# Gated mixer of a 13-stage block: the scores of two heads side by side over 64 rows each, in two banks of their own; squares moved to GpSimd

## The chip, the cores and the metric

One core of a Trainium2 chip runs the whole program. The metric is the device time of one execution in microseconds (us), a median over runs. One core has TensorE (PE: matmuls; PEld is its loading of weights), VectorE (DVE), ScalarE (ACT), GpSimd (POOL) and SyncE (SP, which only issues transfers here). Each engine works through its own list of instructions in order and waits on semaphores that others raise.

## The reference, cut to what matters

The model is two blocks of two layers on a stream of 256 tokens by 1024 features, all in float32: eight feed-forward stages, four mixers and one key/value stage. The change is in one mixer, the gated one (`mlstm`):

```
H, L = 8 heads, chunks of 64 tokens; q, k: 64 wide per head, v: 128 wide per head
q, k, v, ig, fg, og = split(h @ w_in);  q = q / 8
log_i = ig + b_if[0];  log_f = log_sigmoid(fg + b_if[1]);  b = cumsum(log_f)
m_t = running maximum of the exponents                  # per token and head
W   = exp(D - m_t) * (q @ k.T)        # D: b[t] - b[s] + log_i[s], causal
num = W @ v (+ the part of earlier chunks);  den = sum(W) (+ the same)
h_out = num / max(|den|, exp(-m_t))
h_out = rmsnorm(h_out over the 128 of a head, g_head)
return (h_out * sigmoid(og)) @ w_out
```

The kernel computes the chunked recurrence as one causal product over all 256 tokens, which is the same sum. For each head: exponents, scores, their elementwise product W, then W times v with a column of ones beside it, which gives the denominator.

## The kernel before

The program is one list of stages (`PHASES`). Large matmuls split each float32 operand in a high and a low part ("fp32r") and make three matmuls of them (`mm3`, lines 540 to 542). Weights come in through a ring of buffers: SyncE loads `raw`, ScalarE makes the high part (`prep`, line 492), VectorE the low part (line 501), and TensorE gives the buffer back through `used`. The order of work on every engine is written out by hand.

In the gated mixer the tokens are two blocks of 128. The causal half of a 256 x 256 matrix has three blocks, so an exponent or score tile is 128 partitions by `TRI` = 384 columns. PSUM banks are called `A[0..3]`, `G[0..1]` and `X[0..1]`, 512 columns each. The arena holds `mls["q"]` and `mls["k"]`: four tiles of 128 rows by 256 tokens, with an even head in rows 0 to 63 and the odd head in rows 64 to 127.

After the projections comes the head loop, which is what the change rewrites:

- **TensorE** (line 1498). For head i: a causal mask into `G[i % 2]` (`masked`, 384 columns), the decay of the head added by two matmuls with `pick_r` (128 and 256 columns), and the scores q·k into `X[i % 2]` (line 1509, 128 and 256 columns). The scores run over all 128 rows: for an even head `mls["k"]` has zeros in rows 64 to 127, for an odd head `k_odd` has zeros in rows 0 to 63. These float32 matmuls appear as two passes each. Then, for head i - 1, `weigh` (lines 1216 to 1218) multiplies W by v into `A[j % 2]`.
- **ScalarE** (line 2146). For head i: `Exp` of the exponents into `PT` (line 2150), which has two buffers; then for head i - 1: copy of the result out of PSUM into `mls["o"]` (line 2157, raises `o_out`) and two `Square` with a row sum (line 2166, raises `ml_sq`).
- **VectorE** (line 2940). For head i: `PT` times the scores (line 2942, raises `w_done`). After head 4 `measure(0)` computes the norm of heads 0 to 3 from `o_out` and `ml_sq` and raises `ml_ms`; GpSimd raises it to the power -1/2 (line 864, `ml_pow`); after head 6 `scale(0)` multiplies the heads by it (line 2918, `ml_y`).
- **TensorE** then transposes heads 0 to 3 (`turn_half(0)`, line 1494, into `A[2]` and `A[3]`) before the last `weigh`. VectorE gates the transposed chunks (`mix(0)`, line 2927, `ml_mix`), ScalarE makes their high parts (`head_hi`, line 2142, `o_hi`), VectorE the low parts (`ml_lo`, line 2605, `o_lo`). `w_out`, the output projection, starts when all heads are out (`o_out` at 8) and chunk 0 has its low part. In its middle stands `turn_half(1)` for heads 4 to 7, which pass through the same steps.

Of the kernel before, what the change touches and what calls it, by code (L numbers as in the profile page):

```python
# [268 lines left out]
def blocks_program(nc, W, out):  # L269
# [6 lines left out]
    with ctx:  # L276
# [80 lines left out]
        PT = cut(work, 0, 2, TRI)  # L357
# [33 lines left out]
        def event(name):  # L391

            if name not in ev:
# [10 lines left out]
        k_odd = cut(work, 768, 4, S)  # L404
# [25 lines left out]
                   bif=stat(2 * ML_H), junk=cut(work, 1792, P), sc=cut(yf, 512, 4, S))  # L430
# [114 lines left out]
        ML_T = ((A[2], A[3]), (G[0], G[1]))  # L545
        KV_C, KV_K = (A[2], A[3], G[0], G[1]), (G[0], G[1], A[1], A[3])
# [222 lines left out]
        def _(pool):  # L769
# [72 lines left out]
            for n, name in enumerate(NORMS):  # L842
# [64 lines left out]
        def _(pe):  # L907
# [541 lines left out]
            def mlstm_mixer():  # L1449
# [36 lines left out]
                pe.wait_ge(tlin_out, tl[0] - 1)  # L1486
# [11 lines left out]
                for i in range(ML_H + 1):  # L1498
                    if i < ML_H:
                        if i >= 2:  # L1500
                            pe.wait_ge(w_done, i - 1)
                        if i == 1:
                            pe.wait_ge(tlin_out, tl[0])
                        q, k = mls["q"][:, i // 2, :], (mls["k"], k_odd)[i % 2][:, i // 2, :]
                        masked(G[i % 2], "causal", True)
                        for at, n, ks, qs in ((0, P, slice(P, S), slice(P, S)), (P, S, slice(0, P), slice(0, S))):
                            mm(G[i % 2][:, at:at + n], pick_r[:, i:i + 1].to_broadcast([P, P]), decay[:, qs],
                               start=False, stop=at == P)
                            last = mm(X[i % 2][:, at:at + n], k[:, ks], q[:, qs], start=True, stop=True)
                        last.then_inc(st_ready, 1)  # L1510
                    if i >= 1:
                        j = i - 1
                        pe.wait_ge(w_done, j + 1)
                        if j >= 2:
                            pe.wait_ge(o_out, j - 1)
                        weigh(A[j % 2], 0, ML_DV + 1, PT[:, j % 2, :], mls["v"][:, :, j, :]).then_inc(pv_done, 1)
                    if i == 7:
                        turn_half(0)
                pe.wait_ge(o_out, ML_H)
# [231 lines left out]
        def _(act):  # L1751
# [348 lines left out]
            def mlstm_mixer():  # L2100
# [36 lines left out]
                w0 = 0  # L2137

# [5 lines left out]
                for i in range(ML_H + 1):  # L2144
                    if i < ML_H:
                        act.wait_ge(st_ready, w0 + i + 1)
                        if i >= 2:
                            act.wait_ge(pv_done, w0 + i - 1)
                        for t, at, n in ((0, P, S), (1, 0, P)):
                            last = A_(PT[:, i % 2, at:at + n], G[i % 2][:, at:at + n], ACT.Exp, bias=mls["R"][:, t, i:i + 1])  # L2150
                        last.then_inc(e_done, 1)
                    if i == ML_H:
                        head_hi(0)
                    if i >= 1:
                        j = i - 1
                        act.wait_ge(pv_done, w0 + j + 1)
# [3 lines left out]
                        act.wait_ge(o_out, j + 1)  # L2160
                        if j == ML_H - 1:
                            head_hi(1)
                        for t in range(NT):
                            if t + j:
                                act.wait_ge(event("ml_sq"), NT * j + t)
                            A_(mls["junk"], mls["o"][:, t, j, 0:ML_DV], ACT.Square, accum_out=mls["ssq"][:, t, j:j + 1]
                               ).then_inc(event("ml_sq"), 1)
                for c in range(2, ML_H):
                    if c == 4:
                        gates((5, 7))  # L2170
                    head_hi(c)
# [1091 lines left out]
```

## Time and profile before

| | us |
|---|---|
| median of 3 runs (1936.01 to 1937.71) | 1937.04 |
| the profiled execution: span from first to last instruction | 1936.5 |
| TensorE busy | 1922.3 |
| VectorE busy | 1189.8 |
| ScalarE busy | 1190.5 |
| GpSimd busy | 392.5 |
| head loop, from its first mask to the first matmul of `w_out` | 1175.40 to 1192.24 |

The profiled execution is known by its span; the 0.5 us up to the median of the three timed runs is within their spread. Times in the views are counted from the first instruction. Matmuls overlap in the view, so the distance between two starts, not a row's length, says what one costs TensorE.

### The profile page before, as it was taken

Reading aid. Unit: us, or ns where it says so; the run is one execution under the profiler, and the core shown is the slowest. Engines: PE = TensorE matmul, PEld = TensorE weight load, DVE = VectorE, ACT = ScalarE, POOL = GpSimd, SP = SyncE. Lnnn points to the kernel's source line nnn. Section 1 sums busy time; section 2 is a strip of 40 time slices with the busy share of each in tenths; the row PEclk is TensorE's granted clock in tenths of the full one; section 3 lists DMA queues with packets and bytes.
Section 4 is the critical chain, followed back from the end, with each engine's and each line's share of the span. In section 5 each row is a group of like instructions: output and inputs, shape, how many; then the busy total and the mean of one; then the engine's idle time right before and its main releaser. Section 6 shows DMA issues by size and latency. Waiting matters only on the chain.

```text
span 1936.5 us, 26905 instructions
## 1 busy us (share of the span) xinstructions
PE 1922.3 (99%) x9518; PEld 1621.1 (84%) x9518; DVE 1189.8 (61%) x1641; ACT 1190.5 (61%) x2147; POOL 392.5 (20%) x717
## 2 busy tenths in 40 slices
PE   9999999999999999999999999999999999999999
PEld 7888988888888898888888898888888888888887
DVE  6655656556655666555755666755576555877554
ACT  7555557555655666555755547755577555766553
POOL 1222302221222002221222100222112221211221
PEclk9999999999999999999999999999999999999999
DMA  9657436564655426665555434655556553306550
GB/s 326 211 189 216 153 110 203 191 194 150 225 191 184 142 76 218 196 195 174 192 193 193 161 131 142 206 195 195 174 172 226 191 194 130 109 21 217 198 195 23
DMA packets 241056, 338.96 MB, mean 175 GB/s; under 512 B 5727, under 2 KB 206350, under 8 KB 240830
## 3 DMA queue, kind: packets, MB, share of 16 engines
q1 hardware_dynamic: 239710, 335.84, 52.8%
q0 software_dynamic: 496, 1.23, 0.3%
q8 instruction: 58, 0.95, 0.2%
q10 hardware_dynamic: 752, 0.61, 0.1%
q14 instruction: 40, 0.33, 0.1%
HBM read 336.61 MB, written 1.05 MB: 174 GB/s over the span
## 4 chain that ended last, share of the span: by engine, by line
PE 94%; DVE 2%; ACT 2%; DMA 1%; issue 1%; POOL 0%; SPq 0%; ACTq 0%; DVEq 0%
PE A L540 11%; PE A L542 11%; PE A L541 11%; PE G L540 10%; PE G L542 10%; PE G L541 10%; PE X L540 8%; PE X L542 8%; PE X L541 8%; PE A L1247 1%; PE A L925 1%; PE X L1231 1%; DVE wl L501 1%; PE G L1259 1%; ACT wh L492 0%
## 5 line engine op out<-in xcount | busy, mean ns | idle before, releaser
L501 DVE TENSOR_TENSOR wl<-raw,wh 128x1024 fp32r<-128x1024 f32 (+1 forms) x553 | 658.4, 1231 | 134.5 <-ACT wh L492 133.6
L492 ACT ACTIVATE wh<-raw 128x1024 fp32r<-128x1024 f32 (+1 forms) x553 | 555.9, 1052 | 179.3 <-PE G L542 73.4
L805 POOL COPY work<-work 32x128 f32<-32x128 f32 x640 | 323.6, 506 | 909.9 <-DVE work L2497 886.6
L540 PE MATMUL G<-wh,xh 128*128 128x512 f32 (+1 forms) x814 | 317.9, 391 | 0.9 <-ACT arena L2267 0.7
L542 PE MATMUL G<-wh,xl 128*128 128x512 f32 (+1 forms) x814 | 316.3, 389 | 0.0
L541 PE MATMUL G<-wl,xh 128*128 128x512 f32 (+1 forms) x814 | 316.1, 388 | 0.0
L540 PE MATMUL X<-wh,xh 128*128 128x512 f32 x672 | 261.7, 389 | 1.1 <-DVE wl L501 1.1
L542 PE MATMUL X<-wh,xl 128*128 128x512 f32 x672 | 261.5, 389 | 0.0
L541 PE MATMUL X<-wl,xh 128*128 128x512 f32 x672 | 261.4, 389 | 0.0
L1832 ACT ACTIVATE work<-work 32x128 f32<-32x128 f32 x640 | 196.5, 307 | 16.1 <-DVE work L2497 9.6
L2502 DVE TENSOR_TENSOR hidl<-work,hidh 128x512 fp32r<-128x512 f32 x80 | 55.4, 692 | 237.8 <-ACT hidh L1838 237.8
L540 PEld LDWEIGHTS G<-wh,xh 128*128 128x128 f32 x814 | 152.8, 188 | 33.2 <-ACT arena L2267 0.8
L542 PEld LDWEIGHTS G<-wh,xl 128*128 128x128 f32 x814 | 152.8, 188 | 31.5
L541 PEld LDWEIGHTS G<-wl,xh 128*128 128x128 f32 x814 | 152.8, 188 | 30.9
L540 PE MATMUL A<-wh,hidh 128*128 128x512 f32 x384 | 150.2, 391 | 0.9 <-DVE hidl L2502 0.8
L541 PE MATMUL A<-wl,hidh 128*128 128x512 f32 x384 | 149.5, 389 | 0.0
L542 PE MATMUL A<-wh,hidl 128*128 128x512 f32 x384 | 149.5, 389 | 0.0
L540 PEld LDWEIGHTS X<-wh,xh 128*128 128x128 f32 x672 | 126.1, 188 | 27.9 <-issue 1.9
L542 PEld LDWEIGHTS X<-wh,xl 128*128 128x128 f32 x672 | 126.1, 188 | 26.3
L541 PEld LDWEIGHTS X<-wl,xh 128*128 128x128 f32 x672 | 126.1, 188 | 26.2
L1838 ACT ACTIVATE hidh<-work 128x512 fp32r<-128x512 f32 x80 | 50.6, 632 | 125.9 <-POOL work L805 125.9
L1815 ACT ACTIVATE work<-G,st 128x256 f32<-128x256 f32 x96 | 40.4, 472 | 141.9 <-PE G L542 141.0
(486 smaller groups left out, 2949.9 us busy)
## 6 DMA issues: line engine op xcount, KB each, us to landing
raw<-in_ffn_w_in SPq DMA_DIRECT2D x88, 1024.0 KB, 6.8
raw<-in_ffn_w_down SPq DMA_DIRECT2D x44, 1024.0 KB, 5.0
raw<-in_ffn_w_out SPq DMA_DIRECT2D x44, 1024.0 KB, 4.9
raw<-in_ffn_w_gate SPq DMA_DIRECT2D x42, 1024.0 KB, 5.5
raw<-in_ffn_w_up SPq DMA_DIRECT2D x42, 1024.0 KB, 7.3
raw<-in_a_w_in SPq DMA_DIRECT2D x12, 1024.0 KB, 5.3
raw<-in_ab_w_in SPq DMA_DIRECT2D x8, 1024.0 KB, 7.0
raw<-in_kv_w SPq DMA_DIRECT2D x6, 1024.0 KB, 5.3
```

The costliest lines, as they stand in the source:

```text
L492: nc.scalar.activation(hi, r, ACT.Copy).then_inc(hi_done[u], 1)
L501: nc.vector.tensor_tensor(lo, r, hi.bitcast(F32), ALU.subtract).then_inc(lo_done[u], 1)
L540: nc.tensor.matmul(o, sh, rh, start=start, stop=False)
L541: nc.tensor.matmul(o, sh, rl, start=False, stop=False)
L542: return nc.tensor.matmul(o, sl, rh, start=False, stop=stop)
L805: last = nc.gpsimd.tensor_copy(*square_views(i, j))
L925: last = nc.tensor.transpose(NB[b][:, i * S + t * P:i * S + (t + 1) * P], h[:, t, c * P:(c + 1) * P], ident)
L1231: last = nc.tensor.transpose(X[n % 2][:, i * P:(i + 1) * P], probs[:, n % 2, i * P:(i + 1) * P], ident)
L1815: A_(silu[:, t, :], GB[b % 2][t][:, 0:S], ACT.Silu, scale=rstd[:, t:t + 1]).then_inc(silu_ready, 1)
L1832: last = A_(*square_views(i, j), ACT.Copy)
L1838: A_(hidh[:, b % 2, :], hid_t, ACT.Copy).then_inc(hidh_done, 2)
L2502: V.tensor_tensor(hidl[:, b % 2, :], hid_t, hidh[:, b % 2, :].bitcast(F32), ALU.subtract).then_inc(hidl_done, 2)
```

## The change

The scores of the heads 2p and 2p + 1 are computed together. `exponents_pair(p)` makes both masks and decays, pairs of heads taking turns between the banks `A[2], A[3]` and `G[0], G[1]` (`ML_G`). `products_pair(p)` makes both heads' scores over 64 rows each, the even head from rows 0 to 63 into `X[0]`, the odd head from rows 64 to 127 into `X[1]`, alternately. So `k_odd` and the zeros in `mls["k"]` are gone, and with them two memsets of VectorE and four of its eight half-height copies of k. `PT` has three buffers, and ScalarE copies a head out one step later. The squares are made by GpSimd into a buffer `mls["sq"]`, and VectorE sums them in `measure` with one `tensor_reduce` over 1024 elements; `measure(0)` stands after head 5 and no longer after head 4. On ScalarE `head_hi(0)` and `head_hi(1)` stand behind the last copy.

```diff
-                for i in range(ML_H + 1):
-                    if i < ML_H:
-                        if i >= 2:
-                            pe.wait_ge(w_done, i - 1)
-                        if i == 1:
-                            pe.wait_ge(tlin_out, tl[0])
-                        q, k = mls["q"][:, i // 2, :], (mls["k"], k_odd)[i % 2][:, i // 2, :]
-                        masked(G[i % 2], "causal", True)
-                        for at, n, ks, qs in ((0, P, slice(P, S), slice(P, S)), (P, S, slice(0, P), slice(0, S))):
-                            mm(G[i % 2][:, at:at + n], pick_r[:, i:i + 1].to_broadcast([P, P]), decay[:, qs],
-                               start=False, stop=at == P)
-                            last = mm(X[i % 2][:, at:at + n], k[:, ks], q[:, qs], start=True, stop=True)
...
+                def exponents_pair(p):
+                    if p >= 2:
+                        pe.wait_ge(e_done, 2 * p - 2)
+                    for i in (2 * p, 2 * p + 1):
+                        bank = ML_G[p % 2][i % 2]
+                        masked(bank, "causal", True)
+                        for at, n, qs in ((0, P, slice(P, S)), (P, S, slice(0, S))):
+                            last = mm(bank[:, at:at + n], pick_r[:, i:i + 1].to_broadcast([P, P]), decay[:, qs],
+                                      start=False, stop=at == P)
+                        last.then_inc(st_ready, 1)
+                def products_pair(p):
+                    if p:
+                        pe.wait_ge(w_done, 2 * p)
+                    for at, n, ks, qs in ((0, P, slice(P, S), slice(P, S)), (P, S, slice(0, P), slice(0, S))):
+                        for odd in range(2):
+                            own = slice(HD * odd, HD * (odd + 1))
+                            last = mm(X[odd][:, at:at + n], mls["k"][own, p, ks], mls["q"][own, p, qs], start=True,
+                                      stop=True)
+                    last.then_inc(st_ready, 1)
...
+                exponents_pair(0)
+                pe.wait_ge(tlin_out, tl[0])
+                products_pair(0)
+                for p in range(ML_H // 2):
+                    more = p + 1 < ML_H // 2
+                    if more:
+                        exponents_pair(p + 1)
+                    weigh_head(2 * p)
+                    if more:
+                        products_pair(p + 1)
+                    else:
                         turn_half(0)
+                    weigh_head(2 * p + 1)
...
+                        for j in range(4 * f, 4 * f + 4):
+                            pool.wait_ge(o_out, j + 1)
+                            o = mls["o"][:, :, j, 0:ML_DV]
+                            nc.gpsimd.tensor_tensor(mls["sq"][:, j % 4, :, :], o, o, ALU.mult).then_inc(event("ml_sq"), 1)
                         part = slice(4 * f, 4 * f + 4)
                         pool.wait_ge(event("ml_ms"), f + 1)
...
-                    dve.wait_ge(event("ml_sq"), 8 * f + 8)
+                    dve.wait_ge(event("ml_sq"), 4 * f + 4)
+                    link(V.tensor_reduce(mls["ssq"][:, :, part], mls["sq"].rearrange("p h t n -> p t h n"),
+                                         AX.X, ALU.add))
...
                     dve.wait_ge(e_done, i + 1)
-                    V.tensor_tensor(PT[:, i % 2, :], PT[:, i % 2, :], X[i % 2][:, 0:TRI], ALU.mult).then_inc(w_done, 1)
+                    dve.wait_ge(st_ready, 3 * (i // 2) + 3)
+                    V.tensor_tensor(PT[:, i % 3, :], PT[:, i % 3, :], X[i % 2][:, 0:TRI], ALU.mult).then_inc(w_done, 1)
...
-                    if i == 4:
+                    if i == 5:
                         measure(0)
```

On TensorE the rows of two heads in the middle of the loop stood like this before (G0 and G1 hold exponents, X0 and X1 scores, A0 and A1 results; the last number is columns):

```order
L1212 MATMUL G1<-const_r 128x384
L1507 MATMUL G1<-const_r 128x128
L1509 MATMUL X1<-arena,work 128x128
L1507 MATMUL G1<-const_r 128x256
L1509 MATMUL X1<-arena,work 128x256
L1216 MATMUL A0<-arena,work 128x129
L1217 MATMUL A0<-arena,work 128x129
L1218 MATMUL A0<-arena,work 128x129
L1212 MATMUL G0<-const_r 128x384
L1507 MATMUL G0<-const_r 128x128
L1509 MATMUL X0<-arena 128x128
```

Now a pair of heads stands like this:

```order
L1216 MATMUL G0<-const_r 128x384
L1509 MATMUL G0<-const_r 128x128
L1509 MATMUL G0<-const_r 128x256
L1216 MATMUL G1<-const_r 128x384
L1509 MATMUL G1<-const_r 128x128
L1509 MATMUL G1<-const_r 128x256
L1220 MATMUL A0<-arena,work 128x129
L1221 MATMUL A0<-arena,work 128x129
L1222 MATMUL A0<-arena,work 128x129
L1520 MATMUL X0<-arena 128x128
L1520 MATMUL X1<-arena 128x128
L1520 MATMUL X0<-arena 128x256
```

The four score matmuls of a pair lie next to one another, alternating between the two banks, and the exponents of a pair come before the `weigh` of the pair ahead.

On VectorE the rows from the multiplication of the second head to the scaling of heads 0 to 3 (`y` holds the small per-token numbers, `arena` the head outputs) were:

```order
L2942 TENSOR_TENSOR work<-work,X 128x384 [waits e_done] x4
L2903 SCALAR_TENSOR_TENSOR y<-arena 128x2x4 [waits o_out]
L2904 TENSOR_TENSOR y<-y 128x2x4 [waits dve_chain]
L2905 RECIPROCAL y<-y 128x2x4 [waits dve_chain]
L2907 TENSOR_TENSOR y<-y 128x2x4 [waits ml_sq,dve_chain]
L2908 TENSOR_TENSOR y<-y 128x2x4 [waits dve_chain]
L2909 TENSOR_SCALAR y<-y 128x2x4 [waits dve_chain]
L2942 TENSOR_TENSOR work<-work,X 128x384 [waits e_done] x2
L2915 TENSOR_TENSOR y<-y 128x2x4 [waits ml_pow]
L2918 TENSOR_TENSOR arena<-arena,y 128x4x128 [waits dve_chain]
L2918 TENSOR_TENSOR arena<-arena,y 128x4x128
L2942 TENSOR_TENSOR work<-work,X 128x384 [waits e_done]
```

Now they are:

```order
L2952 TENSOR_TENSOR work<-work,X 128x384 [waits st_ready,e_done] x5
L2910 SCALAR_TENSOR_TENSOR y<-arena 128x2x4 [waits o_out]
L2911 TENSOR_TENSOR y<-y 128x2x4 [waits dve_chain]
L2912 RECIPROCAL y<-y 128x2x4 [waits dve_chain]
L2914 TENSOR_REDUCE y<-work 128x2x4 [waits ml_sq,dve_chain]
L2916 TENSOR_TENSOR y<-y 128x2x4 [waits dve_chain]
L2917 TENSOR_TENSOR y<-y 128x2x4 [waits dve_chain]
L2918 TENSOR_SCALAR y<-y 128x2x4 [waits dve_chain]
L2952 TENSOR_TENSOR work<-work,X 128x384 [waits st_ready,e_done]
L2924 TENSOR_TENSOR y<-y 128x2x4 [waits ml_pow]
L2927 TENSOR_TENSOR arena<-arena,y 128x4x128 [waits dve_chain]
L2927 TENSOR_TENSOR arena<-arena,y 128x4x128
L2952 TENSOR_TENSOR work<-work,X 128x384 [waits st_ready,e_done]
```

The measuring of heads 0 to 3 has moved behind one more multiplication and has a reduction in its middle; the multiplication of head 6 stands behind it, where heads 5 and 6 did.

On ScalarE the rows from the last `Exp` to the first high parts (`mh`) of the output projection were:

```order
L2150 ACTIVATE work<-G,y 128x256 [waits pv_done,st_ready]
L2150 ACTIVATE work<-G,y 128x128
L2157 ACTIVATE arena<-A 128x2x129 [waits pv_done]
L2166 ACTIVATE work,y<-arena 128x128 [waits ml_sq,o_out]
L2166 ACTIVATE work,y<-arena 128x128 [waits ml_sq]
L2142 ACTIVATE mh<-y 128x256 [waits ml_mix]
L2157 ACTIVATE arena<-A 128x2x129 [waits pv_done]
L2142 ACTIVATE mh<-y 128x256 [waits ml_mix,o_out]
L2166 ACTIVATE work,y<-arena 128x128 [waits ml_sq] x2
```

Now they are:

```order
L2173 ACTIVATE work<-G,y 128x256 [waits pv_done,st_ready]
L2173 ACTIVATE work<-G,y 128x128
L2179 ACTIVATE arena<-A 128x2x129 [waits pv_done]
L2173 ACTIVATE work<-G,y 128x256 [waits pv_done,st_ready]
L2173 ACTIVATE work<-G,y 128x128
L2179 ACTIVATE arena<-A 128x2x129 [waits pv_done] x3
L2165 ACTIVATE mh<-y 128x256 [waits ml_mix] x4
```

The squares are gone, and the first high part no longer stands ahead of the last copy but behind it.

## Rows read from the trace of the kernel before

**Rows 1.** The page: span, TensorE's busy time, granted clock by slice.
```profile
span 1936.5 us, 26905 instructions
...
PE 1922.3 (99%) x9518; PEld 1621.1 (84%) x9518; DVE 1189.8 (61%) x1641; ACT 1190.5 (61%) x2147; POOL 392.5 (20%) x717
...
PEclk9999999999999999999999999999999999999999
```

**Rows 2.** All waits of TensorE from 1095 to 1250 us, two of three.
```profile
PE A L540 <- ACT arena L2157: 0.5, 1, 0.5
PE A L1494 <- DVE arena L2918: 0.5, 1, 0.5
```

**Rows 3.** Timeline of TensorE: start us, length us, engine, line, out<-in, xcount.
```profile
1175.40 0.34 PE L1212 MATMUL G<-const_r 128*128 128x384 f32 x1
...
1180.46 0.42 PE L1212 MATMUL G<-const_r 128*128 128x384 f32 x1
1180.72 0.22 PE L1507 MATMUL G<-const_r 128*128 128x128 f32 x1
1180.78 0.44 PE L1509 MATMUL X<-arena,work 128*128 128x128 f32 x2
1180.97 0.36 PE L1507 MATMUL G<-const_r 128*128 128x256 f32 x1
1181.17 0.59 PE L1509 MATMUL X<-arena,work 128*128 128x256 f32 x2
1181.60 0.42 PE L1216 MATMUL A<-arena,work 128*128 128x129 f32 x2
...
1182.23 0.42 PE L1212 MATMUL G<-const_r 128*128 128x384 f32 x1
...
1190.01 1.09 PE L1494 MATMUL A<-const,arena 128*128 128x128 f32 x8 [0.47 <-DVE arena L2918]
...
1192.24 0.50 PE L540 MATMUL A<-wh,mh 128*128 128x512 f32 x1 [0.48 <-ACT arena L2157]
```

**Rows 4.** Timeline of ScalarE, head loop and its end.
```profile
1180.18 0.72 ACT L2150 ACTIVATE work<-G,y 128x256 f32<-128x256 f32 x2
...
1181.95 0.72 ACT L2150 ACTIVATE work<-G,y 128x256 f32<-128x256 f32 x2
...
1191.81 0.39 ACT L2157 ACTIVATE arena<-A 128x258 f32<-128x258 f32 x1 [0.17 <-PE A L1218]
1192.22 0.42 ACT L2142 ACTIVATE mh<-y 128x256 fp32r<-128x256 f32 x1
```

**Rows 5.** Timeline of VectorE, head loop.
```profile
1179.05 0.55 DVE L2942 TENSOR_TENSOR work<-work,X 128x384 f32<-128x384 f32 x1
...
1186.08 0.17 DVE L2909 TENSOR_SCALAR y<-y 128x8 f32<-128x8 f32 x1
...
1188.65 1.29 DVE L2918 TENSOR_TENSOR arena<-arena,y 128x512 f32<-128x512 f32 x2
```

**Rows 6.** Timeline of GpSimd in the same stretch.
```profile
1186.33 1.65 POOL L864 TENSOR_TENSOR y<-y,const 128x8 f32<-128x8 f32 x1 [82.88 <-DVE y L2909]
```

**Rows 7.** Groups by form: xcount | busy us, mean ns | idle before.
```profile
L3085 DVE TENSOR_REDUCE st<-arena 128x8 f32<-128x512 f32 x4 | 2.7, 678 | 0.0
...
L835 POOL TENSOR_SCALAR arena<-arena 128x256 f32<-128x256 f32 x4 | 4.2, 1060 | 0.2
...
L879 POOL TENSOR_TENSOR arena<-arena,st 128x256 f32<-128x256 f32 x4 | 2.5, 616 | 37.0 <-DVE st L3122 37.0
```

**Rows 8.** Timeline of TensorE around the 8-column matmuls of line 1475.
```profile
1120.89 0.61 PE L1475 MATMUL A<-const,y 128*8 128x128 f32 x8
1121.43 0.39 PE L540 MATMUL G<-xh,wh 128*128 128x256 f32 x1
```

**Rows 9.** Timeline of TensorE at the start of the program.
```profile
1.30 3.78 PE L913 MATMUL X<-y 128*128 128x128 f32 x16 [1.30 <-DVE arena L3202]
...
7.91 0.66 PE L925 MATMUL A<-const,h 128*128 128x128 f32 x4 [1.75 <-DMA h<-in_x]
```

More of the change, by code:

```diff
@@ L355, in blocks_program @@
         hid, squares_t, hid_t = cut(work, 4 * S, 2, S), cut(work, 2 * S, 2 * S), cut(work, 6 * S, 2 * S)
-        PT = cut(work, 0, 2, TRI)
+        PT = cut(work, 0, 3, TRI)
         x_landed = [sem(f"x_landed{part}") for part in range(3)]
@@ L403, in blocks_program @@
         small_t = cut(work, 2048, S)
-        k_odd = cut(work, 768, 4, S)
         decay = masks_r["chunk64"][:, 0:S]
@@ L429, in blocks_program @@
                    d=cut(yf, 192, NT, 8), m=cut(yf, 208, NT, 8), top=cut(yf, 512, 2, P + S), li=cut(yf, 1280, S),
-                   bif=stat(2 * ML_H), junk=cut(work, 1792, P), sc=cut(yf, 512, 4, S))
+                   bif=stat(2 * ML_H), sq=cut(work, 3 * TRI, 4, NT, ML_DV), sc=cut(yf, 512, 4, S))
         final = dict(by=cut(arena, 0, D), y=cut(arena, D, NT, D), ss=mla["ss"][:, 0, :], ms=mla["ms"][:, 0, :],
@@ L545, in blocks_program @@
         ML_T = ((A[2], A[3]), (G[0], G[1]))
+        ML_G = ((A[2], A[3]), (G[0], G[1]))
         KV_C, KV_K = (A[2], A[3], G[0], G[1]), (G[0], G[1], A[1], A[3])
@@ new lines, in weigh_head @@
+                def weigh_head(j):
+                    pe.wait_ge(w_done, j + 1)
+                    if j >= 2:
+                        pe.wait_ge(o_out, j - 1)
+                    weigh(A[j % 2], 0, ML_DV + 1, PT[:, j % 3, :], mls["v"][:, :, j, :]).then_inc(pv_done, 1)
+                exponents_pair(0)
[9 more added lines that the diff above has]
+                    else:
@@ L2136, in mlstm_mixer @@
                 prep("mlstm", 9, (1, 2))
-                w0 = 0
                 def head_hi(c):
@@ L2142, in head_hi @@
                     A_(mh[:, c, :], mls["sc"][:, c % 4, :], ACT.Copy).then_inc(o_hi, 1)
-                for i in range(ML_H + 1):
+                for i in range(ML_H + 2):
                     if i < ML_H:
-                        act.wait_ge(st_ready, w0 + i + 1)
-                        if i >= 2:
-                            act.wait_ge(pv_done, w0 + i - 1)
+                        act.wait_ge(st_ready, 3 * (i // 2) + i % 2 + 1)
+                        if i >= 3:
+                            act.wait_ge(pv_done, i - 2)
                         for t, at, n in ((0, P, S), (1, 0, P)):
-                            last = A_(PT[:, i % 2, at:at + n], G[i % 2][:, at:at + n], ACT.Exp, bias=mls["R"][:, t, i:i + 1])
+                            last = A_(PT[:, i % 3, at:at + n], ML_G[i // 2 % 2][i % 2][:, at:at + n], ACT.Exp,
+                                      bias=mls["R"][:, t, i:i + 1])
                         last.then_inc(e_done, 1)
[L2152 to L2156, printed above, removed]
+                    if i >= 2:
+                        j = i - 2
+                        act.wait_ge(pv_done, j + 1)
                         A_(mls["o"][:, :, j, :], A[j % 2][:, 0:2 * (ML_DV + 1)].rearrange("p (t n) -> p t n", t=NT),
                            ACT.Copy).then_inc(o_out, 1)
[L2160 to L2168, printed above, removed]
+                for c in range(ML_H):
                     if c == 4:
@@ L2834, in evac @@
                     for e in TLIN["mlstm"][first:first + count]:
-                        if e[2] == "k":
-                            tlin_evac("mlstm", e, mls["k"][0:HD, e[3], :], rows_=slice(0, HD))
-                            last = tlin_evac("mlstm", e, k_odd[HD:P, e[3], :], rows_=slice(HD, P))
-                        else:
-                            last = tlin_evac("mlstm", e, mls[e[2]][:, e[3], :], ML_DK ** -0.5 if e[2] == "q" else 1.0)
-                        last.then_inc(tlin_out, 1)
+                        tlin_evac("mlstm", e, mls[e[2]][:, e[3], :], ML_DK ** -0.5 if e[2] == "q" else 1.0
+                                  ).then_inc(tlin_out, 1)
                         tl[0] += 1
```

18 lines of the change are left out of this document (4 added, 14 removed).

## The prediction

> **What bounds the kernel now.** I read the page first: TensorE is busy for 1922.3 of 1936.5 us [rows 1], so only a microsecond that TensorE works less or waits less can count. The waits of TensorE over the whole mixer and beyond come next: there are three in 155 us, and the two largest, of 0.5 each, stand at the end of the head loop, one for the scaling of heads 0 to 3 and one for the last copy [rows 2]. All before the loop is therefore hidden behind TensorE: the two memsets and the four spare copies that VectorE loses are worth 0.
>
> The timeline of TensorE then gives the loop: first mask at 1175.40, `turn_half(0)` at 1190.01, `w_out` at 1192.24 [rows 3], in all 16.84 us. This is the only stretch that can change. One head costs 1182.23 - 1180.46 = 1.77 us: mask and decay 0.26 + 0.06 + 0.20 = 0.52, scores 0.19 + 0.43 = 0.62, `weigh` 0.63. The reader is to see that no row has an idle time behind it. But ScalarE goes round in the same time: the `Exp` of two heads start 1181.95 - 1180.18 = 1.77 apart [rows 4]. Both engines bound the loop at once, and behind the loop there is a third bound, a chain through VectorE and GpSimd.
>
> **The change part by part.**
>
> *Scores side by side.* The row-split matmul itself is not in the trace of before. The nearest is line 1475: 8 passes of 128 columns, whose results lie in two separate 32-partition strips. From 1120.89 to the next matmul at 1121.43 they take 0.54 us [rows 8], the way out of this mode included. `weigh` has 6 passes of 129 columns in 0.63 [rows 3], at which pace 8 would take 0.83. So two parts of the array did work beside each other, split by columns there and by rows here. A pair has 2 heads x 2 passes x 384 = 1536 columns: at the pace of line 1475 it takes 0.54 x 1.5 = 0.81, and I take 0.85 with the way in. If nothing overlaps it is 2 x 0.62 = 1.24, and with changes of mode 1.3: that is the other bound.
>
> The Trainium skill, "TensorEngine Tiling (Array Packing)", sections Theoretical Speedup and Key Properties, gives up to twice the rate for a contraction of 64 rows, but says that every change of tiling mode drains TensorE. By the first alone a pair would cost 0.62, and the sum below would be 0.5 us lower; the row on line 1475 shows the gain and also that it is less than twofold.
>
> *Exponents.* Six matmuls of one kind in a row no longer alternate with another kind. Per head 0.52 is the upper bound, and I take 0.45, so 0.90 for a pair.
>
> *ScalarE* loses the squares: a head costs it one pair of `Exp` (0.72) and one copy (0.39) [rows 4], 1.1 and no longer 1.77. It leaves the race.
>
> *TensorE up to the fourth head.* Multiplication 1 of VectorE still stands behind the 1024-element `prep` and ends where it did, at 1179.05 + 0.55 = 1179.60 [rows 5]. `products_pair(1)` waits for it, since its banks come free only then; TensorE has done exponents 2 and 3 and `weigh` of head 0 by about 1178.8 and stands idle for 0.9 us, which is new. From 1179.70 on nothing waits: products 0.85, `weigh` 1 0.63, exponents 4 and 5 0.90, `weigh` 2 0.63, products 0.85, `weigh` 3 0.63, together 4.49, to 1184.19. Before, `weigh` 2 ended at 1182.23 [rows 3] and `weigh` 3 one round later, at 1184.00. It is not earlier, though TensorE works less, because more has been put ahead of it.
>
> *The chain behind head 3.* The result is out of the array 0.25 after a block's end, the copy starts 0.04 later and takes 0.39 [rows 4]: 1184.87. GpSimd squares 256 elements: 0.62 by its multiplication of that shape (line 879) [rows 7]; 1.06 is the other end (line 835) [rows 7]. With 0.08 to start, 1185.57. The reduction over 1024 elements has no row: 512 cost 0.678 (line 3085) [rows 7] and 512 more about 0.6 (two scalings of 512 in 1.29) [rows 5], so 1.28: 1186.90 with its start. Three small operations as before, the last one being the 0.17 of line 2909: 1187.50. In the profile of before that one starts at 1186.08 [rows 5] and GpSimd's power at 1186.33 [rows 6]; now the power starts at 1187.58, 1.25 later, and takes 1.65 again: 1189.23. The small product and the scaling take 0.03 + 0.19 + 1.29, the signal 0.06: `turn_half(0)` starts at 1190.80 and not at 1190.01. That is **+0.8 us**. Part of the 1.25 is absorbed because before, the power was ready at 1186.33 + 1.65 = 1187.98, 0.5 us before VectorE came to it.
>
> The Trainium skill, "GPSIMD Engine Reference", section Key points, speaks against this move: GpSimd shares its memory interfaces with VectorE and contends with instructions of two SBUF inputs. By that rule a square would rather cost the 1.06 of line 835, 0.44 us more.
>
> What TensorE does meanwhile: `weigh` 6 needs multiplication 6, which now stands behind `measure(0)`, so it starts at about 1188.1 and ends at 1188.7; then TensorE is idle until 1190.80, for 2.1 us. All that the scores save ends here.
>
> *From `turn_half(0)` to `w_out`.* Before: 2.23 us (1190.01 to 1192.24), ended by the last copy [rows 2 to 4]. The copy starts 1191.81 - 1190.01 = 1.80 after the transposes. Now the high part of chunk 0 stands behind that copy on ScalarE: 1.80, 0.33 until ScalarE takes it up, 0.42 for it (the row at 1192.22) [rows 4], 0.03 and 0.42 for the low part on VectorE, 0.05 for the signal: 3.05 us. That is another **+0.8 us**. Queued behind it are the gatings of chunks 2 and 3, which `w_out` needs only from its 7th and 13th matmul on.
>
> *Later.* `turn_half(1)` needs the second scaling; GpSimd's squares 4 to 6 are done by then, and square 7 follows the last copy. I find the second scaling ready about 0.6 us before TensorE asks for it; before it was 1.7. No new wait, but little cover.
>
> *Sum:* 0.8 + 0.8 = +1.6 us on a span of 1936.5, so 1938.1; on the median of 1937.04 it is **1938.6 us**. 0.2% of the time is 3.9 us, about what a measurement of this kernel can tell from no change. The forecast is no change that can be told.
>
> **The rivals.**
>
> *1. The scores do not run side by side.* For it: no row here splits the array by rows. Against: line 1475. Products cost 1.3, so two blocks ahead of `weigh` 3 add 0.9, and the first block another 0.3 because multiplication 0 waits for it: +2.8 us, 1939.8.
>
> *2. The chain behind head 3 does not bind.* Then TensorE's own work counts: from 1179.70 three products (2.55), six `weigh` (3.78) and two pairs of exponents (1.80) end at 1187.83, and `w_out` starts 3.05 later at 1190.88: -1.4 us, 1935.7. It needs a chain 3 us shorter than I have added up; a square and a reduction at half their price would give 1.
>
> *3. TensorE's clock falls, and the kernel is slower.* Between 1188.7 and 1193.8 TensorE has two waits of 2.1 and 1.5 us with 1.55 us of work between. The granted clock stands at its upper level (2.4 GHz) in all slices of the page [rows 1], though at the start of the program 16 passes of 128 columns take 3.78 us, over 0.2 each against 0.11 in `weigh`, which is the pace of the lower level (1.2 GHz) [rows 9]. A wait of 1.75 us behind four passes did not bring it back: the passes at 7.91 are at full pace [rows 9]. If it falls in the second wait and stays down for 3.8 us again, half of that is lost: +1.6 + 1.9 = +3.5 us, 1940.5. It decides (over 3.9) if the low stretch is longer than 4.6 us.
>
> The Trainium skill, "TensorE: Matmul & The Clock Gate", Part 1, says that the slow state is the default and that activity releases it, which is the mechanism of this rival.
>
> **How the numbers follow.** Chances: forecast 0.62, rival 1 0.18, rival 2 0.08, rival 3 0.12. The forecast's own range is 1937.8 (products 0.62, the reduction 0.3 cheaper) to 1939.3 (square 1.06, exponents 0.52). With rival 1 and the lower part of rival 3, and 0.5 us for the spread of a median, it is 1936.8 to 1940.8. Slower by over 0.2%: half of rival 3, and rival 1 with the dear square, 0.11. Faster by over 0.2% would need -3.9 us out of a stretch in which all cases give back at most 1.4: 0.03 for what I have not seen. Within 0.2%: 0.86.
>
> **What the profile will show.** Right: passes of the two banks of a pair starting in twos; a wait of TensorE of about 0.9 for multiplication 1; the power of GpSimd at about 1187.6; a wait of about 2 us at `turn_half(0)`, released by the scaling; a wait of 1.3 to 1.5 at `w_out`, released by a low part and not by a copy; `w_out` near 1193.8. Wrong: `turn_half(0)` before 1190 (rival 2), a products block of 1.2 (rival 1), a granted clock under 1 behind 1190 (rival 3), or a new wait at `turn_half(1)`.

## The result, and the profile after

The changed kernel takes 1944.25 us (median of 5 runs, 1942.49 to 1945.54) against 1937.38 of the kernel before on the same chip (5 runs, 1936.01 to 1939.04): a ratio of 1.0034 with a 95% interval of 1.0024 to 1.0045. That is slower by 6.9 us, more than can be taken for no change, and 3.5 us above the range of the prediction.

The profiled execution has a span of 1940.8 us and a device time of 1942.62; between the two lie 1.8 to 1.9 us, in every run of either kernel. (What stands ahead of the prediction took the 0.5 us between the span of one execution and the median of others for spread; the two are not the same measure.) These are three lines of its page, to be read like [rows 1]:

```profile
span 1940.8 us, 26877 instructions
...
PE 1923.0 (99%) x9518; PEld 1621.5 (84%) x9518; DVE 1189.9 (61%) x1637; ACT 1184.8 (61%) x2115; POOL 397.5 (20%) x725
...
PEclk9999999999999999999999999999999999999999
```

The page hides the matter: a slice of it is 48.5 us long, and the granted clock reads 9 in all. The waits of TensorE from 1095 to 1250 us show more. Before there were three, the largest 0.5 [rows 2]:

```profile
PE A L1497 <- DVE arena L2927: 3.0, 1, 3.0
PE A L539 <- DVE ml L2618: 1.5, 1, 1.5
PE X L1520 <- DVE work L2952: 0.7, 1, 0.7
PE A L1220 <- DVE work L2952: 0.6, 1, 0.6
```

The same stretch in the timeline of TensorE, to be read beside [rows 3]:

```profile
1174.91 0.34 PE L1216 MATMUL A<-const_r 128*128 128x384 f32 x1
...
1179.19 0.93 PE L1520 MATMUL X<-arena 64*128 64x128 f32 x8 [0.66 <-DVE work L2952]
1180.04 0.49 PE L1220 MATMUL A<-arena,work 128*128 128x129 f32 x2
...
1180.73 0.42 PE L1216 MATMUL A<-const_r 128*128 128x384 f32 x1
...
1181.63 0.38 PE L1220 MATMUL A<-arena,work 128*128 128x129 f32 x2
...
1191.91 1.97 PE L1497 MATMUL A<-const,arena 128*128 128x128 f32 x8 [3.04 <-DVE arena L2927]
1193.67 0.64 PE L1220 MATMUL A<-arena,work 128*128 128x129 f32 x2
...
1196.71 0.47 PE L539 MATMUL A<-wh,mh 128*128 128x512 f32 x1 [1.54 <-DVE ml L2618]
```

`turn_half(0)` starts 17.00 us after the first mask (14.61 before) and `w_out` 21.80 (16.84 before). The row of the eight transposing passes is 1.97 long, where it was 1.09 [rows 3]. The windows say why. Each line has the stretch, its length, the busy time of PE, PEld, DVE, ACT and POOL in it, then PEclk, the granted clock (1.00 is the upper level), and the load of the DMA queues.

```profile
1188.00:1190.00 2.00, 0.86 (x6) 0.67 (x6) 0.80 (x2) 0.39 (x1) 2.00 (x3) 1.00 0.56 182
1190.00:1191.00 1.00, 0.00 (x0) 0.00 (x0) 1.00 (x2) 0.00 (x0) 1.00 (x2) 1.00 0.02 6
1191.00:1192.00 1.00, 0.09 (x1) 0.10 (x2) 1.00 (x2) 0.00 (x0) 0.30 (x1) 0.89 0.00 0
1192.00:1193.00 1.00, 1.00 (x5) 1.00 (x6) 0.32 (x1) 0.00 (x0) 0.00 (x0) 0.50 0.00 0
1193.00:1195.00 2.00, 2.00 (x11) 1.87 (x9) 0.88 (x2) 0.00 (x0) 0.00 (x0) 0.50 0.00 0
1195.00:1196.00 1.00, 0.17 (x1) 0.00 (x0) 0.07 (x1) 0.79 (x3) 0.33 (x1) 0.91 0.00 0
```

TensorE does nothing from 1191.91 - 3.04 = 1188.87; near the end of that wait the clock falls to its lower level (1.2 GHz, PEclk 0.50), and it is back at the upper one (2.4 GHz) behind 1195. A mean of 0.89 over one us is 0.22 us at the lower level, one of 0.91 is 0.18, and between them lie 3 us: the low stretch is 3.4 us long.

VectorE in the same stretch. The first three rows belong to the measuring of heads 0 to 3, ahead of the power; the two scalings have a row each:

```profile
1184.84 0.47 DVE L2911 TENSOR_TENSOR y<-y 128x8 f32<-128x8 f32 x1
1185.35 0.20 DVE L2912 RECIPROCAL y<-y 128x8 f32<-128x8 f32 x1
1185.59 1.22 DVE L2914 TENSOR_REDUCE y<-work 128x8 f32<-128x1024 f32 x1
...
1189.17 0.57 DVE L2924 TENSOR_TENSOR y<-y 128x8 f32<-128x8 f32 x1 [1.30 <-POOL y L868]
1189.77 1.06 DVE L2927 TENSOR_TENSOR arena<-arena,y 128x512 f32<-128x512 f32 x1
1190.76 1.10 DVE L2927 TENSOR_TENSOR arena<-arena,y 128x512 f32<-128x512 f32 x1
...
1195.93 0.63 DVE L2618 TENSOR_TENSOR ml<-y,mh 128x256 fp32r<-128x256 f32 x1 [1.99 <-ACT mh L2165]
```

And GpSimd; the first row is the square of head 3:

```profile
1184.68 0.61 POOL L865 TENSOR_TENSOR work<-arena 128x256 f32<-128x256 f32 x1 [1.11 <-ACT arena L2179]
...
1187.49 1.65 POOL L868 TENSOR_TENSOR y<-y,const 128x8 f32<-128x8 f32 x1 [2.20 <-DVE y L2918]
1189.11 0.61 POOL L865 TENSOR_TENSOR work<-arena 128x256 f32<-128x256 f32 x1
1189.67 0.61 POOL L865 TENSOR_TENSOR work<-arena 128x256 f32<-128x256 f32 x1
1190.24 1.06 POOL L865 TENSOR_TENSOR work<-arena 128x256 f32<-128x256 f32 x1
...
1195.67 0.61 POOL L865 TENSOR_TENSOR work<-arena 128x256 f32<-128x256 f32 x1 [4.37 <-ACT arena L2179]
```

Read the two fences against each other. As soon as the power is done, GpSimd goes on to the squares of heads 4 to 6, which have waited behind it, just when VectorE starts to scale. The small product starts at 1189.17 and ends at 1189.74, 0.02 behind the first square (1189.72). The first scaling starts at 1189.77 and ends at 1190.83, 0.55 behind the second square (1190.28). The third square is on from 1190.24 and ends 0.47 behind that scaling; the second scaling ends 0.56 behind the third square (1191.30). The two engines take turns, each instruction waiting for the other's to end. The two scalings take 2.08 instead of 1.29 [rows 5]. The low part at 1195.93 runs beside the square of head 7 and is longer too (0.63; before 0.42). And it happens once more, ahead of the power: the small product at 1184.84 starts beside the square of head 3, ends 0.02 behind it (1185.31 against 1185.29) and takes 0.47, where the same product took 0.17 before and takes 0.17 in e3, which has no squares on GpSimd.

### The profile page after: what moved, and what is told of

The parts are those of the page before. It is cut to its first block, busy times and chain, and to the rows that moved or that the text cites. A ratio compares the mean times of both kernels' runs of the same rounds, so it can differ in the third digit from the quotient of the medians.

```text
span 1940.8 us, 26877 instructions
## 1 busy us (share of the span) xinstructions
PE 1923.0 (99%) x9518; PEld 1621.5 (84%) x9518; DVE 1189.9 (61%) x1637; ACT 1184.8 (61%) x2115; POOL 397.5 (20%) x725
## 4 chain that ended last, share of the span: by engine, by line
PE 93%; DVE 3%; ACT 2%; issue 1%; DMA 1%; POOL 0%; SPq 0%; ACTq 0%; DVEq 0%
PE A L539 11%; PE A L541 11%; PE A L540 11%; PE G L539 10%; PE G L541 10%; PE G L540 10%; PE X L539 8%; PE X L541 8%; PE X L540 8%; PE A L1251 1%; PE A L929 1%; PE X L1235 1%; DVE wl L500 1%; PE G L1263 1%; ACT wh L491 1%
```

## The experiments

Eight kernels ran in two sets of four; each set had one chip and its own runs of the kernel before (set 1: 1937.02 us, 33 runs; set 2: 1937.40, 30 runs). In the table T is the start of `turn_half(0)`, W that of `w_out` and T2 that of `turn_half(1)`, all in us from the first mask in the profiled execution; the last column is its mean granted clock.

| kernel | set | median us (runs) | ratio to before, 95% | T | W | T2 | clock |
|---|---|---|---|---|---|---|---|
| before | | | | 14.6 | 16.8 | 25.2 | 1.000 |
| changed | | 1944.25 (5) | 1.0034 [1.0024, 1.0045] | 17.0 | 21.8 | 30.1 | 0.999 |
| e5 changed, again | 2 | 1943.52 (8) | 1.0028 [1.0017, 1.0039] | 17.0 | 21.5 | 32.6 | 0.997 |
| e1 squares held | 1 | 1940.70 (11) | 1.0019 [1.0010, 1.0028] | 15.8 | 20.2 | 29.8 | 0.998 |
| e2 wait filled | 1 | 1939.52 (11) | 1.0014 [1.0005, 1.0023] | 17.0 | 20.3 | 28.6 | 1.000 |
| e3 squares on ScalarE | 1 | 1941.01 (11) | 1.0023 [1.0014, 1.0032] | 14.9 | 18.8 | 28.7 | 0.999 |
| e4 high part first | 1 | 1940.82 (11) | 1.0022 [1.0012, 1.0031] | 17.0 | 20.5 | 28.8 | 0.999 |
| e6 chain only | 2 | 1938.96 (11) | 1.0008 [0.9999, 1.0017] | 15.8 | 18.1 | 26.4 | 1.000 |
| e7 head after head | 2 | 1939.81 (11) | 1.0011 [1.0002, 1.0020] | 17.0 | 20.3 | 28.6 | 1.000 |
| e8 reordered | 2 | 1936.50 (11) | 0.9995 [0.9986, 1.0004] | 14.1 | 16.5 | 24.8 | 1.000 |

The first mask itself starts between 1173.5 and 1175.6 us in these profiles, before the change can act in the loop, and the rest of the program behind `turn_half(1)` takes 734.6 to 735.9. So a single span is worth no more than a microsecond or two; the three columns leave this out. The intervals are 0.0009 to 0.0011 wide on each side, or 1.7 to 2.1 us: e1 to e4, e6 and e7 cannot be ranked by them, and e6 and e8 cannot be told from the kernel before.

**e1_hold_squares.** The squares of heads 4 to 7 wait until the scaling of heads 0 to 3 is done. If the two engines get in each other's way, VectorE must return to its old durations.

```diff
                     for f in range(2):
+                        if f:
+                            pool.wait_ge(event("ml_y"), 2)
                         for j in range(4 * f, 4 * f + 4):
```

> The changed kernel with one wait added: GpSimd begins the squares of heads 4 to 7 only when the scaling of heads 0 to 3 is finished. All work is done. Times from the loop's first mask, in the changed kernel: turn_half(0) at 17.0 us, w_out at 21.8. Theory A (the squares of GpSimd slow VectorE's scaling from 1.29 to 2.08 and the small product ahead of it from 0.17 to 0.57; the wait so lengthened lets the clock fall): turn_half(0) at 15.8, the wait ahead of it 1.9 and not 3.0, granted clock 1.00 throughout, w_out at 18.9, span 2.9 us shorter than the changed kernel's, timed 3 to 5 us faster. Theory B (the slow scaling has another cause): both rows unchanged, nothing gained. Theory C (the clock falls because too little is done in the stretch, whatever the longest wait): 1.2 us gained and the transposes still at 0.21 us a pass.

Timeline of VectorE:

```profile
1188.89 0.17 DVE L2926 TENSOR_TENSOR y<-y 128x8 f32<-128x8 f32 x1 [1.30 <-POOL y L870]
1189.09 1.29 DVE L2929 TENSOR_TENSOR arena<-arena,y 128x512 f32<-128x512 f32 x2
1190.30 0.55 DVE L2954 TENSOR_TENSOR work<-work,X 128x384 f32<-128x384 f32 x1
```

The durations are back (0.17 and 1.29), `turn_half(0)` comes 1.2 us earlier, and TensorE waits 1.9 instead of 3.0, all as expected. Also, the multiplication at 1190.30, which reads one operand from PSUM, runs beside a square of GpSimd (from 1190.46) and keeps its 0.55. But the clock, expected at 1.00, falls all the same, and for longer, and `w_out` comes at 20.2 and not at 18.9. Its windows:

```profile
1190.00:1191.00 1.00, 0.56 (x5) 0.57 (x6) 0.84 (x2) 0.00 (x0) 0.54 (x1) 0.96 0.00 0
1191.00:1193.00 2.00, 2.00 (x11) 1.98 (x9) 0.88 (x2) 0.00 (x0) 1.21 (x3) 0.50 0.00 0
1193.00:1195.00 2.00, 0.46 (x3) 0.21 (x2) 0.96 (x3) 0.99 (x3) 0.61 (x1) 0.50 0.00 0
1195.00:1197.00 2.00, 2.00 (x5) 1.61 (x6) 1.92 (x8) 1.88 (x3) 0.00 (x0) 0.50 0.00 0
1197.00:1200.00 3.00, 3.00 (x13) 2.39 (x12) 1.73 (x4) 0.94 (x3) 1.08 (x1) 0.88 0.00 0
```

0.1 + 6 + 0.7 is a low stretch of 6.8 us, over the second wait and into `w_out`. Of its 11 runs four have a mean clock that reads 1.000 (spans 1935.7 to 1938.0) and seven less (down to 0.997, spans 1938.5 to 1941.2). The shortest low stretch in any profile here, 3.4 us, already makes the mean 0.999, so the clock of the same program falls in some executions and not in others, and for a varying time.

**e2_filled_wait.** Nothing is changed but that TensorE works in its long wait: 12 products of the identity with itself into a bank that nobody reads.

```diff
                     else:
+                        for _ in range(12):
+                            mm(X[0][:, 0:P], ident, ident, start=True, stop=True)
                         turn_half(0)
```

> The changed kernel with 12 extra 128x128 float32 matmuls (about 2.6 us) into a free bank in TensorE's wait ahead of turn_half(0); they change no result. Theory A (the clock falls in that wait, and this costs most of what the profile does not explain by chains): the scaling stays slow and turn_half(0) stays at 17.0 us from the first mask, but its transposes take 0.11 a pass and not 0.21, w_out comes 3.2 after it and not 4.8, span 1.6 us shorter, and the timed runs, whose clock is lower than the profiled one's, gain 2 to 5 us. Rival (the clock is a small matter, the chain is all): within 0.5 us of the changed kernel, which would be 1944.

```profile
1187.33 2.84 PE L1543 MATMUL X<-const 128*128 128x128 f32 x24
1190.54 1.09 PE L1497 MATMUL A<-const,arena 128*128 128x128 f32 x8 [0.37 <-DVE arena L2929]
1191.47 0.39 PE L1220 MATMUL A<-arena,work 128*128 128x129 f32 x2
...
1193.84 0.47 PE L539 MATMUL A<-wh,mh 128*128 128x512 f32 x1 [1.54 <-DVE ml L2620]
```

In this timeline of TensorE the transposes start at 17.0 as ever, since the scaling is still slow, but all passes are at full pace, and `w_out` follows after 3.30 instead of 4.80: 1.5 us. The wait of 1.54 ahead of `w_out` stands as it was, and behind it the clock is not low. The granted clock reads 1.00 in every window from 1186 to 1198, and the kernel is 2.5 us over before, not 6.9 (6.1 in e5). The products change no result and shorten no chain, so what they bring back is the clock's: in this stretch it falls because of the long wait. (One of the 11 runs reads 0.999, so a fall somewhere in the program is not ruled out.)

**e3_scalar_squares.** The pairs stay, but squares and row sums go back to ScalarE; the reduction falls away (the same edit puts the old count back in `measure`).

```diff
-                        for j in range(4 * f, 4 * f + 4):
-                            pool.wait_ge(o_out, j + 1)
-                            o = mls["o"][:, :, j, 0:ML_DV]
-                            nc.gpsimd.tensor_tensor(mls["sq"][:, j % 4, :, :], o, o, ALU.mult).then_inc(event("ml_sq"), 1)
...
+                        act.wait_ge(o_out, j + 1)
+                        for t in range(NT):
+                            if t + j:
+                                act.wait_ge(event("ml_sq"), NT * j + t)
+                            A_(mls["junk"], mls["o"][:, t, j, 0:ML_DV], ACT.Square, accum_out=mls["ssq"][:, t, j:j + 1]
+                               ).then_inc(event("ml_sq"), 1)
```

> The changed kernel with the squares and row sums back on ScalarE, behind each copy, and no reduction on VectorE: the paired scores alone. All work is done. Theory A (squares on GpSimd and their reduction lengthen the chain from head 3 to turn_half(0) by about 1 us and the contention by 1.2): GpSimd's power starts 1 us earlier, turn_half(0) at 14.8 us from the first mask (before: 14.6), no fall of the clock; squares of head 7 stand ahead of the first high part, so w_out 3.9 later, at 18.7; time about 1939, 1 to 2 us above the kernel before. Rival (the paired scores themselves are what costs, for instance by their change of mode): still above 1942.

```profile
PE A L539 <- DVE ml L2621: 2.2, 1, 2.2
PE A L1493 <- DVE arena L2928: 1.6, 1, 1.6
```

These are its two long waits. `turn_half(0)` at 14.9 and `w_out` at 18.8 came as expected (14.8 and 18.7), but the kernel is 2 us slower than expected: here the second wait is the longer one, and the clock falls 0.7 us behind its end, for 3.4 us (windows 0.96 over 1192 to 1194, 0.50 over 1194 to 1196, 0.69 over 1196 to 1198), so that the first half of `w_out` takes 9.9 us and not 8.3. So the squares' place on GpSimd is not the whole cause; pairs with squares on ScalarE lose as well.

**e4_high_part_first.** ScalarE makes the high part of chunk 0 ahead of the last copy again.

```diff
                         j = i - 2
+                        if j == ML_H - 1:
+                            head_hi(0)
                         act.wait_ge(pv_done, j + 1)
...
-                for c in range(ML_H):
+                for c in range(1, ML_H):
```

> The changed kernel with the first high part ahead of the copy of head 7 on ScalarE, as before; the second stays behind it. All work is done. Theory A (the end of the stretch is lengthened by the order on ScalarE): w_out waits for the copy again and comes 3.8 us after turn_half(0) and not 4.8, since the clock is still low there: 1 us gained, 1943. Rival (VectorE's low part is late for another reason): nothing gained.

The wait ahead of `w_out` is the old one, 0.47 for the last copy, and T to W is 3.54 instead of 4.80 or 4.46. The wait of 3.04 and the low clock stay (0.88 over 1190 to 1192, 0.50 over 1192 to 1194, 0.77 over 1194 to 1196: again 3.4 us). The median is 3.8 us over before, 2.3 to 3.1 nearer to it than the changed kernel, where 1 us was expected. Its 11 runs read 0.998 or 0.999 and none lower, so by their clocks the low stretches were shorter too with the second wait gone: the causes do not simply add up in the medians.

**e5_changed_again.** The changed kernel without an edit, because the low stretch of its one profile explains 1.5 of 6.9 us only.

> The changed kernel itself, on the chip and beside the runs of the kernel before that the other three of this set share. Theory A (the clock falls in the wait ahead of turn_half(0) in every run, but how much of the low stretch meets work differs from run to run): a median of 1942 to 1944.5, the runs spread over 3 us or more, the transposes at 0.21 a pass. If it came within 1 us of the kernel with the filled wait (1939.5), the clock would be a small matter after all.

```profile
1190.00:1191.00 1.00, 0.00 (x1) 0.01 (x1) 1.00 (x2) 0.00 (x0) 0.39 (x1) 1.00 0.00 0
1191.00:1193.00 2.00, 2.00 (x11) 2.00 (x12) 1.28 (x3) 0.00 (x0) 0.00 (x0) 0.60 0.00 0
1193.00:1195.00 2.00, 0.92 (x5) 0.63 (x3) 0.32 (x1) 0.99 (x3) 0.58 (x1) 0.50 0.00 0
1195.00:1197.00 2.00, 1.54 (x4) 1.28 (x5) 2.00 (x6) 1.24 (x3) 0.04 (x1) 0.50 0.00 0
1197.00:1200.00 3.00, 3.00 (x9) 2.32 (x8) 2.29 (x8) 1.58 (x3) 0.43 (x1) 0.50 0.00 0
1200.00:1202.00 2.00, 2.00 (x7) 1.57 (x6) 0.71 (x2) 0.00 (x0) 1.22 (x1) 0.59 0.00 0
```

By the windows of this profile the same program is at the lower level from 1191.4 to 1201.6, for 10.2 us, and `turn_half(1)` follows `w_out` after 11.2 us instead of 8.3. A low stretch of 3.4 us makes the mean clock 0.999, one of 6.8 (e1) 0.998, one of 10.2 makes it 0.997. The five timed runs of the changed kernel read 0.999, 0.997, 0.998, 0.996 and 0.997: the profiled execution was the mildest. Of the eight runs of e5 one reads 1.000; it took 1941.29, the others 1941.76 to 1944.25.

**e6_chain_only.** Squares held, eight filling products, high part first: e1, e2 and e4 at once. What is left should be the longer chain from head 3 to the power.

> The changed kernel with three of the earlier edits together: squares of heads 4 to 7 held until the scaling is done, 8 extra matmuls into a free bank in the wait ahead of turn_half(0), and the first high part ahead of the last copy. What is left is the longer chain from head 3 to turn_half(0) alone. From the first mask: turn_half(0) at 15.8 us (before: 14.6), w_out 2.3 later at 18.1 (before: 16.84), no clock under 1. Sum of causes: +1.2 us, 1938.2. If the four causes (chain, contention, order on ScalarE, clock) were not all, it would stand above 1939.5.

T 15.8, W 18.1, as expected; no wait is over 0.7, and the granted clock is 1.00 in all windows of the stretch (three of its 11 runs have a mean of 0.999, so it may still fall in some; so have 4 of the 30 runs of the kernel before in this set). It is 1.6 us over before in the median, where the loop alone would say 1.2; the interval just holds 1.

**e7_head_after_head.** e2 with the four score matmuls of a pair in another order: both of the even head, then both of the odd one. In the program's order of TensorE, with - for e2's order and + for this one:

```order
-L1520 MATMUL X<-arena 128x128 x2
-L1520 MATMUL X<-arena 128x256 x2
+L1520 MATMUL X<-arena 128x128
+L1520 MATMUL X<-arena 128x256
+L1520 MATMUL X<-arena 128x128
+L1520 MATMUL X<-arena 128x256
```

> The kernel with the filled wait, and the four score matmuls of a pair in another order: both of the even head, then both of the odd head, and no longer in turns. All work is done. If TensorE keeps a queue for each half of the rows, passes still start in twos and the block of a pair stays at 0.86 us, time as with the filled wait (1939.5). If it takes passes strictly in program order, the odd head can only begin beside the last pass of the even head: the block grows to about 1.15, turn_half(0) comes 0.6 to 0.9 later, 1940.3.

```profile
1179.92 0.93 PE L1520 MATMUL X<-arena 64*128 64x128 f32 x8 [0.66 <-DVE work L2954]
1180.79 0.49 PE L1220 MATMUL A<-arena,work 128*128 128x129 f32 x2
```

The timeline shows the block as long as before, 1180.79 - 1179.92 = 0.87 (0.85 in the changed kernel), and its passes still start in twos, 0.013 us apart: first the four of 128 columns, then the four of 256, though the program has 128, 256, 128, 256. The alternation in the source is not what sets the heads side by side.

**e8_reordered.** What the others pointed to: pairs with side-by-side scores, squares on ScalarE, both `weigh` of a pair before the next products, both last `weigh` before `turn_half(0)`, a fourth `PT` buffer, and `prep` and `scale(0)` each behind the later multiplication. In the core:

```diff
-        PT = cut(work, 0, 3, TRI)
+        PT = cut(work, 0, 4, TRI)
...
                     weigh_head(2 * p)
+                    weigh_head(2 * p + 1)
                     if more:
                         products_pair(p + 1)
                     else:
                         turn_half(0)
-                    weigh_head(2 * p + 1)
...
-                    if i == 6:
+                    if i == 7:
                         scale(0)
```

> A version made from the findings, all work done: scores in pairs as in the changed kernel; squares on ScalarE as before; both weigh of a pair ahead of the next pair's scores, so that head 3 is out earlier and both last weigh lie ahead of turn_half(0); four PT buffers; the prep that stood between multiplications 0 and 1 behind both. From the first mask: head 3 out of TensorE at 7.2 us, turn_half(0) at 13.3, w_out 2.1 later at 15.4 (before: 16.84); TensorE waits of 0.9 for multiplication 6 and 1.2 ahead of w_out, no fall of the clock: 1.4 us faster than before, 1935.6. If pairing costs TensorE something not seen so far, it stays at or above 1937. If the clock falls with waits of this length too, 1937 to 1939.

```profile
PE A L539 <- DVE ml L2619: 1.3, 1, 1.3
PE A L1216 <- DVE work L2951: 0.7, 1, 0.7
PE A L1493 <- DVE arena L2926: 0.3, 1, 0.3
```

By its waits the long one at `turn_half(0)` is gone, the clock reads 1.000 in all 11 runs, and the kernel is 3.3 us under e7 and 0.9 under before. The interval holds 1, so this is no shown gain; 1935.6 was expected. T comes 0.8 later than expected (14.1 against 13.3). In the trace GpSimd's power is done at 1187.59, but `scale(0)` stands behind multiplication 7, and the multiplications 6 and 7 wait until 1186.91 for the scores of the last pair, to which TensorE comes at 1185.87 with no wait on the way from 1176.28; the scaling starts at 1188.04. W hangs on ScalarE, which is busy without a gap from 1181.4 to 1191 with exponents, copies and squares and only then makes the first high part.

## Why the prediction was wrong, step by step

Two steps failed. The scaling was added at 0.19 + 1.29 us and took 0.57 + 2.08; and the clock was in the sum at nothing, where it cost some 2 to 4 us. Without the clock's share the kernel would have stayed in the stated range: with the wait filled (e2) it is 2.5 us over before, which is 1939.9 beside 1937.38. It is the clock that carries it past 1940.8.

- **Scores side by side, 0.85 a pair:** right, 1179.19 to 1180.04. Rival 1 is out. The Trainium skill, "TensorEngine Tiling (Array Packing)", section Theoretical Speedup, gives up to twice the rate, which would be 0.62 here; the trace gives 0.85. Inside the block the rate is twofold (the second two passes of 128 columns take 0.11 together, two of 256 take 0.22); about 0.1 us is lost behind the first two passes and as much behind the last. The `weigh` behind the block takes 0.69 (1180.04 to 1180.73) and the one ahead of it 0.75 (1181.63 to 1182.38), instead of 0.63.
- **Exponents, 0.90 a pair:** right, 1180.73 to 1181.63.
- **A new wait for multiplication 1:** right in kind, 0.66 and not 0.9.
- **The chain behind head 3:** right in kind. Square 0.61 and reduction 1.22 came as costed (0.62, 1.28). The power starts 12.58 behind the first mask; predicted were 12.18. Of the 0.40 some 0.23 are the three dearer `weigh` next to row-split blocks. As much again is the small product at 1184.84, which took 0.47 beside the square of head 3: the reduction (1185.59) starts 0.04 behind the end of the reciprocal that follows this product, but 0.30 behind the end of the square. The cheaper reduction gives 0.06 back. e6, which has this step and not the next two, puts T at 15.8: +1.2 instead of +0.8.
- **The scaling, 0.19 + 1.29:** this step failed. It takes 0.57 + 2.08, because squares 4 to 6 start with it: +1.2 us, shown by e1. The prediction weighed the contention for the square of head 3 and priced it at 0.44; that square stayed at 0.61, and it was VectorE's small product beside it that grew. That three squares queue up behind the power and are released with the scaling, it did not see, though it named them. The Trainium skill, "GPSIMD Engine Reference", section Key points, says that GpSimd contends with instructions of VectorE that have two SBUF inputs. The trace agrees: the scalings and the small products have two and grew, the multiplication with an operand from PSUM did not. The rule was applied to the wrong instruction.
- **`turn_half(0)` to `w_out`, 3.05:** nearly right. With the clock up it is 3.30 (e2); 0.21 of the rest is the low part beside the square of head 7. With the high part first it is 2.24 (e6), as before. So ScalarE's order costs 1.06, of which 0.21 are that low part, where 0.8 was said.
- **No new wait at `turn_half(1)`:** right.
- **Rival 3, the clock:** it was held too unlikely (0.12) and too cheap. It fell in all of the profiles that have an unfilled wait of 1.85 us or more in this stretch (changed, e1, e3, e4, e5), at the end of the wait or up to 0.7 us behind it, and in none whose longest one there was 1.54 or less; in all but e3 that was the first of the two waits, not the second as the rival had it. The low stretch that the rival priced, 3.8 us, was near the mildest case: 3.4 us with 1.5 lost in the first profile, 10.2 with about 4 lost in e5 (1.2 in T to W against e2, 2.9 in W to T2). In the medians the clock cost 6.9 (or 6.1, e5) over before less the 2.5 of e2: 3.6 to 4.4 us, with intervals of about 2 us on either side. The one run of e5 that reads 1.000 is 2.2 below the median of its set and still above all 11 runs of e2, so the clock may have cost less than that, and the filling may have done more than hold it up. The argument that a wait of 1.75 us at the start did not bring it back [rows 9] was weak: e1 shows that one program falls in some executions and not in others. The Trainium skill, "TensorE: Matmul & The Clock Gate", Part 1, which has activity release the fast state, was on the right side.

In the first profile the account closes: W was predicted at 18.45 behind the first mask; 0.40 for the later power, 1.17 for the scaling, 0.25 between T and W and 1.50 of clock make 21.77, measured 21.80. In the medians the chain alone (e6) is +1.6, the contention at the scaling and ScalarE's order together +0.9 (e2 over e6, from two sets), the clock +3.6 to 4.4; each of these is a difference that the intervals do not settle to a microsecond.

What stays open: the columns give 2.2 us for contention and order, the medians 0.9, and e7's 2.4 stand against 3.4 in its profile. The start of the first mask varies by 2 us between profiles, and whether the changed kernel reaches it earlier on average was not measured. Why the low stretch is short in one execution and long in the next was not found, nor where the clock falls in the runs of e2, e6, e7 and the kernel before that read 0.999. No experiment takes the pairs alone without both other moves and with the clock secured, so what side-by-side scores give by themselves is known only from e8, which also changes the order.

## What to carry to other kernels

When work is taken from TensorE ahead of a chain that it cannot outrun, ask what the clock does in the wait that appears: here a wait that grew from 0.5 to 3.0 us brought a slow stretch behind it that cost as much again as the wait had added, or more, and filling it with matmuls that nobody reads was the single edit with the best median. When work is moved to an engine because that engine is idle, look at what it is released by: squares that become free at the moment when a critical instruction of VectorE with two SBUF operands starts are not hidden. And read the timed runs' clocks, not only one profile: here one profile showed 1.5 of the 2 to 4 us that the clock cost in the median.

## What the runs showed of the hardware

- GpSimd's and VectorE's elementwise instructions with both operands in SBUF took turns instruction by instruction: of three squares of 0.61 the one that started behind a scaling became 1.06, a scaling of 0.65 (half of 1.29) became 1.06 to 1.10, a small product of 0.17 became 0.57 or 0.47, ending 0.02 behind the square. A VectorE multiplication with one PSUM operand kept its 0.55. The Trainium skill, "Trainium Architecture — The Big Picture", section What this means for kernel authors, calls it an exclusive lock, and the ends of the instructions here agree.
- Low stretches of TensorE's clock lasted 3.4, 6.8 or 10.2 us, the same program showing different ones; it was low in none of the profiles whose longest unfilled wait in this stretch was 1.54 us or less, nor behind one of 1.75 at the start of the kernel before.
- TensorE ran matmuls on the two row halves side by side though both of one half stood first in the program: their passes started 0.013 us apart (e7).
